# Attention probabilities of 43 steps transposed by DMA transposition on SyncE's queue, in place of TensorE transpositions and PSUM moves

## The chip, the cores and the metric

The kernel runs on the 8 cores of one Trainium2 chip, one sequence of the batch on each core, with no exchange between them. The time of a run is the device time of the slowest core in microseconds. Each core has TensorE (matmuls and transpositions), VectorE, ScalarE, GpSimd, and SyncE, which only issues DMA transfers here. GpSimd issues transfers too, mainly the weight loads, which round float32 to bfloat16 on the way.

## The reference

Two layers on x of shape (8, 2048, 1024). The change touches the attention of the first layer alone: three head groups with dilations 1, 4 and 16, four heads of 128 each.

```python
sc = jnp.einsum("brnqhe,brnkhe->brnhqk", qb, kk) * (e ** -0.5)   # (B, dil, nb, H, Q, 2Q)
...
sc = jnp.where(mask[None, None, :, None], sc, NEG_INF)
m = jnp.max(sc, axis=-1, keepdims=True)
ex = jnp.exp(sc - m)
den = jnp.sum(ex, axis=-1)                                           # (B, dil, nb, H, Q)
o = jnp.einsum("brnhqk,brnkhe->brnqhe", ex, vv) / jnp.moveaxis(den, -1, -2)[..., None]
```

Each query block of 128 positions looks at its own block of keys and the one before it. Beside the attention the layer has a gated causal convolution over 31 taps, and both feed one output projection. Then come a layer norm, a SwiGLU, an embedding, and a second layer with a short convolution.

## The kernel before

The attention is worked off in six units of two heads and one head group, and each unit in eight steps of two query blocks: 48 steps, a = 0 to 47. A step is scores(a) on TensorE into the PSUM pair PD[2], the mask and row minimum on VectorE (L1215 and L1221, in masked), four exponentials on ScalarE into Pb (L937), the transposition of P on TensorE into PSUM bank PTB[0] (transpose_p, L618), a move of it into PTt on ScalarE (steps in P_ON_ACT, L947) or VectorE (the other 16, L1233), outputs(a) on TensorE (L636), which multiplies with V, and u_move on ScalarE (L968), after which SyncE stores the block to scr (store_u, L1811). A step with two blocks of 256 keys has 8 tiles of 128x128 to transpose; a step of the group with dilation 16, or of first blocks, has 4; steps 0 and 40 have 6.

Around the steps, TensorE projects the queries, keys and values of the next unit (project, L559 and L586), whose rotary embedding is done by VectorE (L1196 to L1200) and GpSimd (L1625). In unit 0 the input of the convolution takes that place (gated, L663); later its transpositions (phases_to_rows L672, conv_back L697) and the convolution (L688). While units 3 to 5 run, the results of three groups are loaded back (load_rows, L1838 to L1845), weighted and added (merge_first L987 on ScalarE, merge L1273 and L1280 on VectorE), and transposed on TensorE (merged_back L648). The statistics go through HBM: ScalarE stores them (scs), SyncE loads them (STL, L1819), and VectorE's weights wait for that.

The order of all this is one list, EVEN, made by even_order: pairs such as ("e", a) for the exponentials, ("t", a) for the transposition, ("o", a) for outputs. Every engine walks through the same list and issues its own part in that order, so a wait holds up all that stands behind it on its engine. In units 1 to 4 the place of step a is: exponentials of a - 1, first half of a projection with outputs of a - 2 in it, second half, transposition of a - 1, scores of a. PTB[0] has one reader at a time: BANK0 lists its users, and each waits (read0) until the one before has been moved out. Pb and PTt have two buffers each.

Weight loads on GpSimd stand in its own program: load_unit for the next unit's projection (L1597), and the output projection's WmixE (L1679), each behind a rotary addition.

Of the kernel before, what the change touches and what calls it, by code (L numbers as in the profile page):

```python
# [19 lines left out]
K = 1024  # L20
# [20 lines left out]
P_ON_ACT = [*range(8, 16), *range(24, 48)]  # L41
# [144 lines left out]
def build():  # L186
# [110 lines left out]
    Pb = sb2("Pb", [128, 4, 256], BF16, off_dg0, 2 * K)  # L297
# [27 lines left out]
    def half(i):  # L325
# [16 lines left out]
    pe_s, dve_ms, dve_mn, act_exp, pe_t, dve_pt, act_pt = (sem(n) for n in (  # L342
        "pe_s", "dve_ms", "dve_mn", "act_exp", "pe_t", "dve_pt", "act_pt"))
# [142 lines left out]
    BANK0 = [u for u in EVEN if u[0] in ("t", "z", "cb", "mb")]  # L486
# [43 lines left out]
    def tensor_program(pe):  # L530
# [77 lines left out]
        def transpose_p(a):  # L608
            if a == 0:
                pe.wait_ge(dve_const, 1)  # L610
            pe.wait_ge(act_exp, 4 * a + 4)
            if a >= 1:
                pe.wait_ge(*read0(("t", a)))
            n = 0
            for bi, blk in enumerate(step_blocks(a)):
                for h in range(2):
                    for c in range(2 if qblock(UNITS[a // 8][1], blk)[0] else 1):
                        mm = pe.transpose(out=PTB[0][:, n * 128:(n + 1) * 128],  # L618
                                          in_=Pb[a % 2][:, 2 * bi + h, c * 128:(c + 1) * 128], identity=ident[:])
                        n += 1  # L620
            mm.then_inc(pe_t, 1)
# [45 lines left out]
        def phases_to_rows(c):  # L667
            if c == 0:
                pe.wait_ge(dve_glu, 16)
            pe.wait_ge(*read0(("z", c)))  # L670
# [55 lines left out]
        def even_mixer():  # L726
            for kind, v in EVEN:
# [8 lines left out]
                elif kind == "t":  # L736
# [168 lines left out]
    def scalar_program(act):  # L905
# [1131 lines left out]
```

## Time and profile before

| what | value |
|---|---|
| median of 3 runs | 1874.15 us (1873.45 to 1919.63) |
| profiled execution | 1876.64 us |
| its span, slowest core (core 2) | 1875.0 us |
| spans of the eight cores | 1864.8 to 1875.0 us |
| TensorE busy | 1768.8 us, 94% of the span |
| VectorE busy | 1076.7 us, 57% |
| ScalarE busy | 541.6 us, 29% |
| GpSimd busy | 292.7 us, 16% |
| transpositions of P on TensorE (L618) | 300, from 93.1 to 499.7 us |
| moves of P: ScalarE L947, VectorE L1233 | 32 and 16 |

The profiled execution has its own time, 1.6 us above its span and 2.5 above the median. The shares are means over the whole program; the change lies between 80 and 460 us of it, so the rows are read there, in windows. In the chain of waits each step is followed back to what released it. The queue q0 (software) carries what GpSimd issues, q1 (hardware) what SyncE issues, q10 what ScalarE issues.

### The profile page before, as it was taken

Reading aid. Unit: us, or ns where it says so; the run is one execution under the profiler, and the core shown is the slowest. Engines: PE = TensorE matmul, PEld = TensorE weight load, DVE = VectorE, ACT = ScalarE, POOL = GpSimd, SP = SyncE. Lnnn points to the kernel's source line nnn. Section 1 sums busy time; section 2 is a strip of 40 time slices with the busy share of each in tenths; the row PEclk is TensorE's granted clock in tenths of the full one; section 3 lists DMA queues with packets and bytes.
Section 4 is the critical chain, followed back from the end, with each engine's and each line's share of the span. In section 5 each row is a group of like instructions: output and inputs, shape, how many; then the busy total and the mean of one; then the engine's idle time right before and its main releaser. Section 6 shows DMA issues by size and latency. Waiting matters only on the chain.

```text
span 1875.0 us, 27051 instructions; the slowest of 8 cores (1864.8 to 1875.0 us)
## 1 busy us (share of the span) xinstructions
PE 1768.8 (94%) x9307; PEld 890.3 (47%) x9488; DVE 1076.7 (57%) x1466; ACT 541.6 (29%) x1059; POOL 292.7 (16%) x304
## 2 busy tenths in 40 slices
PE   6998989988679999999999999999899999999998
PEld 2566656555334444444444444444344444444443
DVE  3455678677695424243486675667824334156668
ACT  2341246567575010101023331113510110101223
POOL 2315443322142000000011100002300000001011
PEclk7999999999799999999999999999999999999999
DMA  9633321735342622132112426113554312330224
GB/s 284 154 66 56 63 59 45 155 105 141 135 115 59 103 40 46 34 65 48 34 23 51 74 49 120 34 34 63 69 88 85 57 23 45 57 57 12 51 74 146
DMA packets 114452, 141.63 MB, mean 76 GB/s; under 512 B 77712, under 2 KB 89104, under 8 KB 111760
## 3 DMA queue, kind: packets, MB, share of 16 engines
q0 software_dynamic: 15120, 63.84, 20.0%
q1 hardware_dynamic: 97568, 74.88, 14.9%
q10 hardware_dynamic: 1632, 1.18, 0.3%
q8 instruction: 80, 1.31, 0.3%
q14 instruction: 52, 0.43, 0.1%
HBM read 168.97 MB, written 19.01 MB: 100 GB/s over the span
## 4 chain that ended last, share of the span: by engine, by line
PE 76%; DVE 9%; issue 5%; DMA 4%; ACT 3%; POOL 1%; SPq 0%; DVEq 0%; ACTq 0%; POOLq 0%
PE pd L812 32%; PE pd L838 16%; PE pd L765 9%; PE pd L856 6%; PE pd L559 4%; PE pd L663 3%; PE pd L586 2%; DVE x_tok L1468 2%; ACT Pb L937 1%; DVE x_tok L1409 1%; DMA xf<-xT 1%; DMA Wt<-conf_conv_we 1%; PE pd L868 1%; DMA xT<-castt 1%; PE pd L602 1%
## 5 line engine op out<-in xcount | busy, mean ns | idle before, releaser
L812 PE MATMUL pd<-xT,ring 128*128 128x512 bf16 x2507 | 553.3, 379 | 10.7 <-DVE hTf L1442 3.2
L812 PEld LDWEIGHTS pd<-xT,ring 128*128 128x128 bf16 x2560 | 249.7, 98 | 310.9 <-issue 11.9
L1071 ACT ACTIVATE sgt<-pd 128x512 f32<-128x512 f32 x176 | 104.9, 597 | 690.4 <-PE pd L812 690.2
L1442 DVE TENSOR_TENSOR hTf<-pd,sgt 128x512 bf16<-128x512 f32 x128 | 88.5, 692 | 345.8 <-ACT sgt L1071 345.8
L838 PE MATMUL pd<-Wfo,hTf 128*128 128x512 bf16 x1003 | 221.1, 379 | 1.1
L1457 DVE TENSOR_TENSOR x_tok<-x_tok,pd 128x1024 f32<-128x1024 f32 x128 | 156.4, 1222 | 57.2 <-PE pd L838 56.7
L559 PE MATMUL pd<-xT,ring 128*128 128x512 bf16 x543 | 175.0, 396 | 11.2 <-DVE xT L1330 5.1
L838 PEld LDWEIGHTS pd<-Wfo,hTf 128*128 128x128 bf16 x1024 | 100.2, 98 | 120.8
L765 PE MATMUL pd<-xT,ring 128*128 128x512 bf16 x502 | 114.8, 383 | 3.7 <-DVE yT L1505 2.6
L856 PE MATMUL pd<-Wpg,x2T 128*128 128x512 bf16 x502 | 115.2, 379 | 0.7 <-DVE sigt L1483 0.2
L1588 POOL DMA_DIRECT2D ring<-ffn_w_in x40 | 21.4, 536 | 603.4 <-PE pd L812 523.7
L1196 DVE TENSOR_TENSOR rt<-pd,rope 128x512 f32<-128x512 f32 x96 | 66.1, 689 | 78.7 <-PE pd L559 32.2
L937 ACT ACTIVATE Pb<-sS,ST 128x256 bf16<-128x256 f32 (+1 forms) x192 | 86.1, 452 | 63.5 <-DVE ST L1221 63.5
L586 PE MATMUL pd<-ring,xT 128*128 128x256 bf16 x384 | 89.0, 277 | 5.3 <-DVE ring L1337 3.4
L559 PEld LDWEIGHTS pd<-xT,ring 128*128 128x128 bf16 x576 | 55.6, 101 | 76.8 <-issue 31.4
L586 PE MATMUL pd<-wx,xT 128*128 128x256 bf16 x384 | 89.1, 273 | 0.9 <-issue 0.2
L1442 DVE TENSOR_TENSOR hTq<-pd,sgt 128x512 bf16<-128x512 f32 x48 | 33.2, 691 | 92.2 <-ACT sgt L1071 92.1
L1625 POOL TENSOR_TENSOR qb<-rt,rt 128x1024 bf16<-128x1024 f32 x24 | 56.6, 2358 | 176.7 <-DVE rt L1200 170.3
L838 PE MATMUL pd<-Wfo,hTq 128*128 128x512 bf16 x376 | 83.8, 379 | 0.4
L765 PEld LDWEIGHTS pd<-xT,ring 128*128 128x128 bf16 x512 | 50.3, 99 | 64.9 <-issue 5.7
L856 PEld LDWEIGHTS pd<-Wpg,x2T 128*128 128x128 bf16 x512 | 49.9, 98 | 61.3 <-issue 2.0
L1625 POOL TENSOR_TENSOR kb<-rt,rt 128x1024 bf16<-128x1024 f32 x24 | 56.6, 2357 | 124.4 <-DVE rt L1200 124.4
(160 smaller groups left out, 2253.7 us busy)
## 6 DMA issues: line engine op xcount, KB each, us to landing
ring<-ffn_w_in POOLq DMA_DIRECT2D x40, 512.0 KB, 5.2
scr<-Ust SPq DMA_DIRECT2D x80, 128.0 KB, 2.0
Wfo<-ffn_w_out POOLq DMA_DIRECT2D x10, 1024.0 KB, 10.4
x_tok<-x SPq DMA_DIRECT2D x16, 512.0 KB, 5.4
out<-x_tok SPq DMA_DIRECT2D x15, 512.0 KB, 2.9
xf<-xT SPq DMA_DIRECT2D x3, 2048.0 KB, 21.9
ring<-even_w_in POOLq DMA_DIRECT2D x9, 512.0 KB, 8.6
La<-scr SPq DMA_DIRECT2D x11, 384.0 KB, 3.4
```

Source lines behind the costliest of these rows:

```text
L559: qk = pe.matmul(half(h % 3), lhsT=wqk[:, d, part * 128:(part + 1) * 128], rhs=xT[:, d, tc * 512:(tc + 1) * 512], start=(d == 0), stop=(d ...
L586: return pe.matmul(half(3)[:, j * 256:(j + 1) * 256], lhsT=xT[:, d, st0:st0 + 127 * dil + 1:dil], rhs=wqkv[3 * (n % 2) + 2][:, d, :], star ...
L765: mm = pe.matmul(bank, lhsT=src[:, d, j2 * 128:(j2 + 1) * 128], rhs=xT[:, d, tc * 512:(tc + 1) * 512], start=(d == 0), stop=(d == 7))
L812: mm = pe.matmul(bank[:, w * 512:(w + 1) * 512], lhsT=w_in[:, d, w * 128:(w + 1) * 128], rhs=xT[:, d, tc * 512:(tc + 1) * 512], start=(d = ...
L838: mm = pe.matmul(bank[:, hf * 512:(hf + 1) * 512], lhsT=ht, rhs=wo[:, hf * 512:(hf + 1) * 512], start=(ff == 0), stop=(ff == nf - 1))
L856: mm = pe.matmul(bank[:, hf * 512:(hf + 1) * 512], lhsT=x2T[t % 2][:, c, :], rhs=Wpg[:, c, hf * 512:(hf + 1) * 512], start=(c == 0), stop= ...
L937: act.activation(out=Pb[a % 2][:, i, 0:nk], in_=sS[a % 2][:, 2 * h + bi, 0:nk], func=AF.Exp, scale=-1.0, bias=ST[:, a // 8, sblk, 2 + h:3 ...
L1071: act.activation(out=sgt[n % 2][:], in_=PD[PAIR[l]["in", f, tc]][:, 0:512], func=AF.Silu).then_inc(act_silu, 1)
L1196: dve.tensor_tensor(out=rt1[:, part, :], in0=bank, in1=rcs[:, 0, cs], op=ALU.mult)
L1442: dve.tensor_tensor(out=ht, in0=PD[PAIR[l]["in", f, tc]][:, 512:1024], in1=sgt[n % 2][:], op=ALU.mult).then_inc(dve_h, 1)
L1457: dve.tensor_tensor(out=xt, in0=xt, in1=bank[:], op=ALU.add).then_inc(dve_acc, 1)
L1625: pool.tensor_tensor(out=(qb, kb)[i % 2][n % 2][:, :, tc * 512:(tc + 1) * 512], in0=rt1[:], in1=rt2[:], op=ALU.add).then_inc(pool_rope, 1)
```

## The change

For steps 0 to 42 the tiles of P are transposed by one DMA transposition per step, from Pb to PTt, issued by SyncE (p_back). TensorE's transpositions and the moves from PSUM are gone for these steps; steps 43 to 47 stay as they were, all moved by ScalarE. P lies packed in Pb, since one DMA takes it whole. outputs(a) now waits for d_pt, the landing of the DMA, and exponentials(a) waits for the landing of step a - 2 before it overwrites Pb. The remaining users of PTB[0] wait for one another only. In SyncE's order p_back(a) stands at the exponentials of its step for a below 33, and behind store_u(a - 2) from 33 on; 260 of the 300 tiles are in these 43 steps.

```diff
-P_ON_ACT = [*range(8, 16), *range(24, 48)]
+P_ON_PE = 43
...
-    Pb = sb2("Pb", [128, 4, 256], BF16, off_dg0, 2 * K)
+    Pb = sb2("Pb", [128, 1024], BF16, off_dg0, 2 * K)
...
-    pe_s, dve_ms, dve_mn, act_exp, pe_t, dve_pt, act_pt = (sem(n) for n in (
-        "pe_s", "dve_ms", "dve_mn", "act_exp", "pe_t", "dve_pt", "act_pt"))
+    pe_s, dve_ms, dve_mn, act_exp, pe_t, act_pt = (sem(n) for n in ("pe_s", "dve_ms", "dve_mn", "act_exp", "pe_t", "act_pt"))
+    d_pt = [sem("d_pt%d" % i) for i in range(2)]
...
-    BANK0 = [u for u in EVEN if u[0] in ("t", "z", "cb", "mb")]
+    BANK0 = [u for u in EVEN if u[0] in ("z", "cb", "mb") or u[0] == "t" and u[1] >= P_ON_PE]
...
     def moved(a):
 
-        return (act_pt, sum(b in P_ON_ACT for b in range(a + 1))) if a in P_ON_ACT else (
-            dve_pt, sum(b not in P_ON_ACT for b in range(a + 1)))
+        return (act_pt, a - P_ON_PE + 1) if a >= P_ON_PE else (d_pt[a % 2], 16 * (a // 2 + 1))
+
+    def columns(a):
+
+        return 128 * sum(4 if qblock(UNITS[a // 8][1], b)[0] else 2 for b in step_blocks(a))
...
         def transpose_p(a):
-            if a == 0:
-                pe.wait_ge(dve_const, 1)
             pe.wait_ge(act_exp, 4 * a + 4)
-            if a >= 1:
-                pe.wait_ge(*read0(("t", a)))
...
+            pe.wait_ge(*read0(("t", a)))
+            transpose_tile(Pb[a % 2], 0, columns(a) // 128).then_inc(pe_t, 1)
...
-                elif kind == "t":
+                elif kind == "t" and v >= P_ON_PE:
                     transpose_p(v)
...
         def exponentials(a):
             act.wait_ge(dve_mn, a + 1)
             if a >= 2:
-                act.wait_ge(pe_t, a - 1)
+                act.wait_ge(*((pe_t, a - 1 - P_ON_PE) if a - 2 >= P_ON_PE else moved(a - 2)))
+            n = 0
...
-                act.activation(out=Pb[a % 2][:, i, 0:nk], in_=sS[a % 2][:, 2 * h + bi, 0:nk], func=AF.Exp, scale=-1.0,
+                act.activation(out=Pb[a % 2][:, n:n + nk], in_=sS[a % 2][:, 2 * h + bi, 0:nk], func=AF.Exp, scale=-1.0,
...
-        def p_move(a):
-            if a in P_ON_ACT:
-                return
-            n = 128 * sum(4 if qblock(UNITS[a // 8][1], b)[0] else 2 for b in step_blocks(a))
-            dve.wait_ge(pe_t, a + 1)
-            if a >= 2:
-                dve.wait_ge(pe_u, a - 1)
-            dve.tensor_copy(out=PTt[a % 2][:, 0:n], in_=PTB[0][:, 0:n]).then_inc(dve_pt, 1)
...
+        def p_back(a):
+
+            sp.wait_ge(act_exp, 4 * a + 4)
+            if a >= 2:
+                sp.wait_ge(pe_u, a - 1)
+                sp.wait_ge(d_pt[a % 2], 16 * (a // 2))
+            n = columns(a)
+            sp.dma_start(out=PTt[a % 2][:, 0:n].rearrange("p (c n) -> p c n", n=128), in_=Pb[a % 2][:, 0:n],
+                         transpose=True).then_inc(d_pt[a % 2], 16)
...
         for kind, v in EVEN:
-            if kind == "o":
+            if kind == "e" and v < 33:
+                p_back(v)
+            elif kind == "o":
                 store_u(v)
+                if 33 <= v + 2 < P_ON_PE:
+                    p_back(v + 2)
```

On TensorE, where the projection of unit 3 ends (L559, L586) and that of unit 4 begins: the transpositions of step 22 (L618, reading Pb), the scores of step 23 (L602), then the transpositions of conv_back (L697, reading Zn). Before:

```order
L586 MATMUL pd<-wx_109,xT 128x256 x5
L618 MATMUL ptb<-ident,Pb_126 128x128 x8
L602 MATMUL pd<-kb_46,qb_44 128x256 x8
L697 MATMUL ptb<-ident,Zn 128x128 x8
L559 MATMUL pd<-xT,ring_104 128x512 x5
L586 MATMUL pd<-ring_106,xT 128x256
```

and in the changed kernel, where the lines are others (project L563 and L590, scores L606, conv_back L693):

```order
L590 MATMUL pd<-wx_109,xT 128x256 x5
L606 MATMUL pd<-kb_46,qb_44 128x256 x8
L693 MATMUL ptb<-ident,Zn 128x128 x8
L563 MATMUL pd<-xT,ring_104 128x512 x5
L590 MATMUL pd<-ring_106,xT 128x256
```

The eight transpositions between the projection and the scores are gone, and conv_back's follow the scores as before.

On SyncE, from the store of step 21 to the loads for the first merges: the stores of Ust (L1811), the statistics (STL), the rows La. Before:

```order
L1811 DMA scr<-Ust_141 128x256 x2
L1819 DMA STL<-scs 128x16x4 x2
L1811 DMA scr<-Ust_142 128x256 x2
L1811 DMA scr<-Ust_143 128x256 x2
L1811 DMA scr<-Ust_141 128x256 x2
L1845 DMA La_67<-scr 128x768
L1845 DMA La_68<-scr 128x768
L1842 DMA La_69<-scr 128x512
```

and in the changed kernel (stores L1796, statistics L1814, rows L1840 to L1838, transpositions L1806):

```order
L1806 DMA_TRANSPOSE PTt_136<-Pb_126 128x8x128
L1796 DMA scr<-Ust_141 128x256 x2
L1806 DMA_TRANSPOSE PTt_137<-Pb_127 128x8x128
L1814 DMA STL<-scs 128x16x4 x2
L1796 DMA scr<-Ust_142 128x256 x2
L1806 DMA_TRANSPOSE PTt_136<-Pb_126 128x4x128
L1796 DMA scr<-Ust_143 128x256 x2
L1806 DMA_TRANSPOSE PTt_137<-Pb_127 128x4x128
L1796 DMA scr<-Ust_141 128x256 x2
L1840 DMA La_67<-scr 128x768
L1840 DMA La_68<-scr 128x768
L1837 DMA La_69<-scr 128x512
```

A transposition of Pb now stands ahead of each store; the one of step 23 is ahead of the statistics' loads, which wait for the stores of ScalarE, and the ones of steps 24 and 25 are behind them.

## Rows read from the trace of the kernel before

**Rows 1.** The page's head: the span of the slowest core.

```profile
span 1875.0 us, 27051 instructions; the slowest of 8 cores (1864.8 to 1875.0 us)
```

**Rows 2.** Busy us by stage: PE, PEld, DVE, ACT, POOL; granted clock, DMA share, GB/s.

```profile
78.00:142.00 64.00, 61.76 (x390) 41.85 (x396) 32.89 (x40) 26.38 (x81) 7.64 (x6) 1.00 0.49 86
208.00:257.00 49.00, 44.29 (x306) 27.71 (x310) 37.12 (x75) 17.74 (x64) 19.45 (x13) 1.00 0.25 55
257.00:352.00 95.00, 91.14 (x698) 62.21 (x712) 73.55 (x111) 56.31 (x144) 31.61 (x18) 0.98 0.34 72
390.00:480.00 90.00, 70.17 (x593) 43.13 (x604) 66.43 (x117) 64.92 (x191) 19.39 (x9) 0.96 0.45 127
```

**Rows 3.** TensorE's timeline, step 21: start us, us, engine, line, operation.

```profile
318.71 0.61 PE L618 MATMUL ptb<-ident,Pb 128*128 128x128 bf16 x8
319.25 1.09 PE L602 MATMUL pd<-kb,qb 64*128 64x256 bf16 x8
```

**Rows 4.** Waits, 257 to 352 us (total, times, longest); a wait in TensorE's timeline.

```profile
PE ptb L697 <- DVE PTt L1233: 2.1, 7, 0.6
...
256.98 0.38 PE L618 MATMUL ptb<-ident,Pb 128*128 128x128 bf16 x4 [2.29 <-ACT Pb L937]
```

**Rows 5.** Landing of 28 x2T transpositions; DMA queues from 1046 to 1050 us.

```profile
DMA to landing us min/median/max: 3.0/3.1/4.2
...
q0 software_dynamic: 174, 0.65, 101.7%
q1 hardware_dynamic: 37, 0.00, 1.0%
xT<-castd SPq DMA_TRANSPOSE x1, 9.5
```

**Rows 6.** Loads issued by GpSimd and transfers beside them (last column: us to landing).

```profile
268.94 1.72 POOL L1597 DMA_DIRECT2D ring<-even_w_in  x3
...
ring<-even_w_in POOLq DMA_DIRECT2D x3, 512.0 KB, 11.4
...
355.24 0.57 POOL L1679 DMA_DIRECT2D WmixE<-even_w_out  x1
...
WmixE<-even_w_out POOLq DMA_DIRECT2D x1, 2048.0 KB, 17.7
scr<-Ust SPq DMA_DIRECT2D x2, 128.0 KB, 16.0
```

**Rows 7.** Steps 15, 23, 26: last exponential L937, outputs L636; scores(26) L602.

```profile
269.93 0.39 ACT L937 ACTIVATE Pb<-sS,ST 128x128 bf16<-128x128 f32 x1
...
276.56 0.39 PE L636 MATMUL ptb<-Vb,PTt 128*128 128x128 bf16 x4
...
332.96 0.49 ACT L937 ACTIVATE Pb<-sS,ST 128x256 bf16<-128x256 f32 x1
...
338.42 0.61 PE L636 MATMUL ptb<-Vb,PTt 128*128 128x128 bf16 x8
349.06 1.15 PE L602 MATMUL pd<-kb,qb 64*128 64x128 bf16 x8
...
355.50 0.39 ACT L937 ACTIVATE Pb<-sS,ST 128x128 bf16<-128x128 f32 x1
...
359.83 0.39 PE L636 MATMUL ptb<-Vb,PTt 128*128 128x128 bf16 x4
```

**Rows 8.** The chain of waits from 330 to 365 us: start us, us, what.

```profile
333.68 9.20 DMA scs<-ST
...
353.49 0.70 DVE ST L1221
...
360.53 0.70 DVE ST L1221
```

**Rows 9.** Busy time from 250 to 270 us, columns as in rows 2.

```profile
250.00:260.00 10.00, 7.71 (x49) 4.39 (x48) 7.72 (x17) 3.09 (x11) 3.06 (x3) 0.92 0.10 35
260.00:270.00 10.00, 9.73 (x64) 6.29 (x65) 7.17 (x14) 4.46 (x18) 5.73 (x4) 0.91 0.08 28
```

More of the change, by code:

```diff
@@ L608, in transpose_p @@
         def transpose_p(a):
-            if a == 0:
-                pe.wait_ge(dve_const, 1)
             pe.wait_ge(act_exp, 4 * a + 4)
-            if a >= 1:
-                pe.wait_ge(*read0(("t", a)))
[L614 to L621, printed above, removed]
+            pe.wait_ge(*read0(("t", a)))
+            transpose_tile(Pb[a % 2], 0, columns(a) // 128).then_inc(pe_t, 1)
         def outputs(a):
@@ L668, in phases_to_rows @@
             if c == 0:
+                pe.wait_ge(dve_const, 1)
                 pe.wait_ge(dve_glu, 16)
-            pe.wait_ge(*read0(("z", c)))
+            else:
+                pe.wait_ge(*read0(("z", c)))
             for i in range(8):
@@ L896, in tensor_program @@
         for i in range(WARM):
-            pe.matmul(PD[2][:, 0:512], lhsT=Pb[1][:, 0, 0:128], rhs=Pb[1][:, 0:2, :].rearrange("p a b -> p (a b)"),
+            pe.matmul(PD[2][:, 0:512], lhsT=Pb[1][:, 0:128], rhs=Pb[1][:, 0:512],
                       start=True, stop=True)
@@ L936, in exponentials @@
                 sblk = st_block(UNITS[a // 8][1], blk)
-                act.activation(out=Pb[a % 2][:, i, 0:nk], in_=sS[a % 2][:, 2 * h + bi, 0:nk], func=AF.Exp, scale=-1.0,
+                act.activation(out=Pb[a % 2][:, n:n + nk], in_=sS[a % 2][:, 2 * h + bi, 0:nk], func=AF.Exp, scale=-1.0,
                                bias=ST[:, a // 8, sblk, 2 + h:3 + h],
                                accum_out=ST[:, a // 8, sblk, h:h + 1]).then_inc(act_exp, 1)
+                n += nk
         def p_move(a):
-            if a not in P_ON_ACT:
-                return
-            n = 128 * sum(4 if qblock(UNITS[a // 8][1], b)[0] else 2 for b in step_blocks(a))
-            act.wait_ge(pe_t, a + 1)
+            n = columns(a)
+            act.wait_ge(pe_t, a - P_ON_PE + 1)
             act.wait_ge(pe_u, a - 1)
@@ L1050, in even_mixer @@
                     exponentials(v)
-                elif kind == "t":
+                elif kind == "t" and v >= P_ON_PE:
                     p_move(v)
@@ L1224, in masked @@
             d.then_inc(dve_mn, 1)
-        def p_move(a):
-            if a in P_ON_ACT:
-                return
-            n = 128 * sum(4 if qblock(UNITS[a // 8][1], b)[0] else 2 for b in step_blocks(a))
-            dve.wait_ge(pe_t, a + 1)
-            if a >= 2:
-                dve.wait_ge(pe_u, a - 1)
-            dve.tensor_copy(out=PTt[a % 2][:, 0:n], in_=PTB[0][:, 0:n]).then_inc(dve_pt, 1)
         def merge_weights(batch):
@@ L1376, in even_mixer @@
                     masked(v)
-                elif kind == "t":
-                    p_move(v)
                 elif kind == "z":
```

1 line of the change is left out of this document (added).

## Prediction

> **What bounds the kernel now.** I first read the span [rows 1]: the profiled execution took 1876.64 us, of which 1875.0 are the span of its slowest core, and the median of the runs shown is 1874.15, so 2.5 less; I sum against 1876.64 and take 2.5 off at the end. All 43 changed steps lie between 80 and 460 us. There the sums by stage [rows 2] show four regimes. From 78 to 142 us (gate and convolution input) TensorE is busy 61.8 of 64 us and VectorE half: TensorE bounds. From 208 to 257 us VectorE works 37 of 49 us with GpSimd beside it, and TensorE stands waiting for exponentials at the end [rows 4]: the rotary chain bounds. From 257 to 352 us TensorE is busy 91.1 of 95 us: it bounds again. From 390 to 480 us TensorE, VectorE and ScalarE have 70, 66 and 65 of 90 us, and none is full: a loop of waits bounds. From 352 to 390 us it is the same kind of loop: the chain of waits goes from one row-minimum (L1221) to the next in 7.04 us by VectorE and ScalarE alone, with no transposition in it [rows 8].
>
> **What the change removes.** 260 of the 300 transpositions leave TensorE, and 43 moves from PSUM leave VectorE (16) and ScalarE (27). Eight transpositions delay the score matmuls behind them by 319.25 - 318.71 = 0.54 us [rows 3], that is 0.0675 us each. Where TensorE bounds this is all gain, where it does not it is nothing:
> - Steps 0 to 5, 46 transpositions before 142 us: 3.1 us.
> - Steps 6 and 7, 16 of them, ahead of the first convolution matmuls: 1.1 us.
> - Steps 8 to 13, 24 of them, under the rotary chain: 0.
> - Steps 14 to 22, 56 of them, TensorE bound: 3.8 us.
> - The conv_back transpositions in that stage waited for the bank that VectorE's move of P still read: 2.1 us over 7 times [rows 4]; the bank is now free: 2.1 us.
> - Step 13's transposition held TensorE 2.29 us for the exponentials [rows 4]. TensorE can now go on with the scores; it bounds from here, so 2.3 us.
> - Steps 23 to 30, 36 of them, under the loop: 0.
> - Steps 31 to 42, 82 of them, and with them the ScalarE moves: between 0 and 5.5 us. The loop runs by VectorE and ScalarE; I take 1.0, near the lower end, since [rows 8] is the nearest row for such a loop and it holds no move.
>
> The sum of the gains is 3.1 + 1.1 + 3.8 + 2.1 + 2.3 + 1.0 = 13.4 us. The removed moves on VectorE and ScalarE are otherwise idle-covered.
>
> **What it adds.** 43 DMA transpositions, on SyncE's queue, each issued when the last exponential of its step is done; outputs(a) on TensorE waits for the landing, and behind that wait stand on TensorE the rest of the projection and the scores two steps on; behind outputs stand u_move on ScalarE, then merge_first, then VectorE's merge and its next mask: everything. exponentials(a) waits for the landing of step a - 2, which is an old one by then. In quiet, such a transposition of 128x1024 lands in 3.0 to 4.2 us, median 3.1 [rows 5]. What is there to cover it is the time from the last exponential to outputs: 276.56 - 270.32 = 6.2 us for step 15, 338.42 - 333.45 = 5.0 for step 23, 359.83 - 355.89 = 3.9 for step 26 [rows 7], less the 0.3 to 0.8 us by which TensorE now comes earlier. So in quiet the landing is hidden, by 0.0 to 2.5 us. In steps 0 to 7 two whole steps of gated blocks lie between, which is more cover than in any later one.
>
> It is not always quiet. While a weight load issued by GpSimd runs, the hardware queues hardly move: in the 4 us from 1046 to 1050 the software queue took 101.7% of the 16 engines with 174 packets, the hardware queue 1.0% with 37, and the transposition then under way landed after 9.5 us [rows 5]. Beside the WmixE load two stores of 128 KB each needed 16.0 us [rows 6]. So I take it that a transposition issued just before or in such a load lands at the load's end. Three steps are hit in the TensorE-bound or loop-bound part:
> - Step 15: last exponential 270.32 [rows 7], loads issued from 268.94 on, the last at about 270.1, landing 11.4 us later at 281.5 [rows 6], and the transposition 1.5 us behind it at 283.0. TensorE would be at outputs(15) at 276.56 less 0.27 for four transpositions and 0.3 for the bank, 276.0: it stalls 7.0 us.
> - Step 23: the scs store issued at 333.68, right behind its exponentials, took 9.20 us beside the next loads, to 342.88 [rows 8]; the transposition then lands at about 343.2. TensorE is at outputs(23) at 338.42 - 0.54 = 337.9: 5.3 us.
> - Step 26: WmixE is issued at 355.24, 0.65 us ahead of the last exponential, and lands after 17.7 us [rows 6], at 372.9. outputs(26) was at 359.83: 13.2 us late.
>
> After a stall the clock is lower: around the 2.29 us wait that ended at 256.98 the mean granted clock was 0.92 from 250 to 260 and 0.91 from 260 to 270 [rows 9], which is (0.08 + 0.09) x 10 = 1.7 us of work lost in a stretch at 1.2 instead of 2.4 GHz. I add 1.7 per stall. Step 15 lies where TensorE bounds: 7.0 + 1.7 = 8.7 us. For step 23, scores(26) moves from 349.06 [rows 7] to 349.06 + 343.2 - 338.42 + 1.7 - 0.5 = 355.0, and ends at 356.2; its mask started 0.7 us before the minimum at 353.49, so 352.8 [rows 8]; the slack was 2.6 us, and the loop slips 3.4. For step 26: 13.2 + 1.7 - 0.3 (its neighbour's transpositions) - 2.6 (the same slack) = 12.0 us. Together 24.1 us. The bounds of this sum are 0 (all three hidden) and, if each lands 3 us later still, 33.
>
> Ahead of step 24's transposition stands, on SyncE, the wait for the scs store and the STL loads; it lands at about 350, when TensorE, late by step 23, has just come to outputs(24). I count nothing for it, but without step 23's stall it would cost what that one does.
>
> **The forecast.** 24.1 - 13.4 = 10.7 us slower: 1887.3 for an execution like the profiled one, 1885 at the median. That is 0.6%, where 2% is about what a measurement of this kernel tells from no change.
>
> **Rivals.**
> First, the load at 269 us misses step 15. Its data starts some 2 us after its issue, and the transposition follows it by only 1.4 us; with four transpositions gone ahead of it, it is 0.3 us earlier still. Against it: the load would have to leave it 3.1 us. Then the sum is 24.1 - 8.7 - 13.4 = +2.0, at the median 1876. Chance 0.18.
>
> Second, the queues share. A transposition of 3.1 us beside a load then takes twice that, 6.2: step 15 lands at 276.5 (0.5 late), step 23 at 339.7 and step 26 at 362.1, late by 1.8 and 2.3, within the slack of 2.6. With one lowered clock the losses are about 2.2 us, the sum is -11.2, and the median comes to 1863. For it: the hardware queue did move some packets beside the load. Against it: 37 packets against 174 [rows 5], and the 16.0 us of the stores [rows 6]. Chance 0.2. The Trainium skill, page "DMA: Bandwidth & Descriptors", section "Issuing engines are not separate DMA queues", says that DMAs from all issuing engines interleave on the same 16 engines, which is this rival; by it the median would be 1863, and [rows 5] and [rows 6] speak against it.
>
> Third, slower by over 2%. From step 8 to step 30 the cover is 3.9 to 6.2 us [rows 7], about 4.5 after TensorE comes earlier. If the ordinary landing, behind the stores of Ust and the loads of La on the same queue, is not 3.1 but 7 us, each of 20 steps stalls 2.5 us: 50 us more, on top of the forecast 1935. It decides from a landing of about 4.5 us on. Against it: all 28 transpositions of x2T landed in 4.2 us or less [rows 5]. Chance 0.06.
>
> That the transpositions stay on TensorE is ruled out by the order of the changed program.
>
> **How the numbers follow.** Forecast (all three stalls) 0.48; first rival 0.18; second 0.2; third 0.06; other mixtures (one stall alone, or two) 0.08, between 1866 and 1882. The range goes from below the second rival, 1861, to the forecast with each landing 3 us later less half the doubt of the gains, 1896; it leaves out the third rival and half of the second's better end. Faster by over 2% would be 1837, which no case reaches: 0.01. Slower by over 2%: 0.06. Within: 0.93.
>
> **What would show it.** Transpositions of P land in 3 to 4 us except those of about steps 8, 15, 23 and 26, which land after 9 to 17 us; TensorE waits for PTt before outputs(15), (23) and (26), the last one some 13 us long, each followed by a stretch at half the granted clock; a step with its two gated blocks, from 78 to 142 us, takes 0.54 us less; conv_back follows the scores with no gap; from 352 us on everything is later than before by about 11 us. The forecast is wrong if no wait for PTt is over 3 us (then the second rival), or if most steps from 8 on wait (the third).

## The result, and the profile after

The changed kernel took 1893.86 us in the median of five runs (1889.92 to 2069.55), the kernel before 1874.15. Runs in which the cores of a die went at a visibly lower clock, like the one of 2069.55 us, are left out of the ratios here and of the medians given below. The ratio is 1.0096, with a 95% interval of 1.0082 to 1.011: about 18 us slower, and within 2%. The profiled execution took 1891.94 us, 15.3 more than the one before; its slowest core is again core 2.

The head of the changed kernel's page, and from the list of its DMA issues the row of the 43 new ones (number, median us to landing):

```profile
span 1889.8 us, 26667 instructions; the slowest of 8 cores (1876.0 to 1889.8 us)
...
PTt<-Pb SPq DMA_TRANSPOSE x43, 3.1
```

The median landing is that of the other transpositions, 3.1 us [rows 5]. So the median says nothing is wrong, and the spread has to be looked at. All instructions on the tile PTt: what TensorE waited for before its outputs (us in all, times), who waited for it, and the spread of the landings:

```profile
  DMA PTt<-Pb: 40.9, 9
...
  PE ptb L630: 42.4, 10
  ACT Ust L964: 27.5, 4
...
DMA to landing us min/median/max: 2.4/3.1/16.0
```

At nine of the 43 steps TensorE waited, 40.9 us together. TensorE's timeline says which (start, us, what; in brackets the idle time ahead and what ended it; L630 is outputs). They are steps 2, 12, 15, 23, 26, 35, 37 and 39; a ninth, of 0.6 us, is left out:

```profile
117.23 1.01 PE L630 MATMUL ptb<-Vb,PTt 128*128 128x128 bf16 x8 [3.76 <-DMA PTt<-Pb]
...
249.51 0.38 PE L630 MATMUL ptb<-Vb,PTt 128*128 128x128 bf16 x4 [2.26 <-DMA PTt<-Pb]
...
281.03 0.59 PE L630 MATMUL ptb<-Vb,PTt 128*128 128x128 bf16 x4 [9.91 <-DMA PTt<-Pb]
...
345.19 1.01 PE L630 MATMUL ptb<-Vb,PTt 128*128 128x128 bf16 x8 [6.04 <-DMA PTt<-Pb]
...
378.22 0.58 PE L630 MATMUL ptb<-Vb,PTt 128*128 128x128 bf16 x4 [10.78 <-DMA PTt<-Pb]
...
440.82 0.61 PE L630 MATMUL ptb<-Vb,PTt 128*128 128x128 bf16 x8 [2.08 <-DMA PTt<-Pb]
...
453.12 0.61 PE L630 MATMUL ptb<-Vb,PTt 128*128 128x128 bf16 x8 [2.33 <-DMA PTt<-Pb]
...
464.24 0.61 PE L630 MATMUL ptb<-Vb,PTt 128*128 128x128 bf16 x8 [3.11 <-DMA PTt<-Pb]
```

Four of them stand in the chain of waits with the whole flight of their DMA (start us, us, what), and each was issued beside weight loads of GpSimd; for step 15 GpSimd's row is the first here:

```profile
266.23 1.72 POOL L1582 DMA_DIRECT2D ring<-even_w_in  x3
```

```profile
100.84 16.04 DMA PTt<-Pb
...
267.15 13.54 DMA PTt<-Pb
...
334.75 10.10 DMA PTt<-Pb
...
363.06 14.81 DMA PTt<-Pb
```

Busy time by stage, to be read against [rows 2] (columns as there):

```profile
78.00:142.00 64.00, 60.24 (x339) 38.14 (x339) 27.68 (x33) 25.05 (x76) 7.64 (x6) 0.97 0.65 107
208.00:257.00 49.00, 45.35 (x283) 25.89 (x282) 37.24 (x78) 16.15 (x60) 17.90 (x10) 0.97 0.33 72
257.00:352.00 95.00, 79.05 (x567) 51.77 (x566) 61.43 (x83) 50.56 (x126) 29.41 (x18) 0.91 0.46 91
390.00:480.00 90.00, 75.07 (x534) 42.43 (x532) 68.59 (x124) 52.08 (x177) 21.21 (x9) 0.94 0.58 127
```

The third line shows it best: TensorE's 91.1 busy us of 95 are now 79.1, and its granted clock 0.91 in place of 0.98. A part of the fall is the transpositions that are gone, the rest comes from the waits of 9.9 and 6.0 us. VectorE, which had nothing taken away in the last stage, is nearly the same there (68.6 and 66.4 us), though the later windows no longer hold quite the same steps.

One core is not enough for sizes of 2 or 3 us. So I took, on each of the eight cores, the start of TensorE's scores of steps 0, 8, 14, 24, 32, 41 and 46 and of the first convolution matmul, and the median of the eight for each stretch between two of them. Names e1 to e12 are the experiments below.

| us, median of 8 cores | steps 0-7 | convolution | 8-13 | 14-23 | 24-31 | 32-40 | 41-45 |
|---|---|---|---|---|---|---|---|
| before | 73.0 | 57.6 | 45.8 | 77.8 | 56.0 | 48.8 | 37.6 |
| after | 70.2 | 56.4 | 45.5 | 80.6 | 73.2 | 48.8 | 36.6 |
| e1 eight steps back | 70.5 | 56.8 | 42.8 | 74.9 | 58.1 | 49.7 | 35.9 |
| e2 four alone | 73.0 | 55.7 | 45.8 | 84.9 | 72.9 | 48.9 | 36.9 |
| e3 paced loads | 69.6 | 56.3 | 42.8 | 73.2 | 59.4 | 50.7 | 35.8 |
| e4 none late | 70.5 | 55.9 | 42.8 | 74.9 | 57.5 | 48.9 | 37.8 |
| e5 0-22, paced | 69.6 | 56.2 | 42.8 | 73.5 | 55.5 | 48.8 | 37.3 |
| e6 0-22, 39-42, paced | 69.6 | 56.2 | 42.8 | 73.5 | 55.9 | 48.6 | 36.2 |
| e7 load shifted | 70.3 | 55.8 | 42.8 | 80.2 | 71.5 | 49.6 | 36.5 |
| e8 four plain copies | 72.9 | 55.9 | 45.8 | 81.9 | 71.7 | 48.9 | 37.5 |
| e9 before, paced | 73.0 | 56.5 | 45.8 | 77.8 | 55.0 | 48.8 | 37.6 |
| e10 unpaced, 23 steps | 70.5 | 57.0 | 42.8 | 74.9 | 56.2 | 48.7 | 36.2 |
| e11 load in 1 KB | 70.4 | 55.7 | 42.8 | 81.5 | 68.9 | 50.5 | 36.2 |
| e12 load in 512 B | 70.8 | 55.6 | 43.8 | 81.9 | 67.2 | 48.8 | 36.7 |

The wait of a step comes two steps later than its scores, so that of step 23 falls in the stretch 24-31. The convolution waits for its own weights too and differs by 1.2 to 6.0 us from core to core within a kernel; nothing is read from it. Without any DMA in its steps, the stretch 24-31 has medians of 55.0 to 56.2 us in five kernels (before, e5, e6, e9, e10), so differences under about 1 us say nothing there. What follows scores(46) differs by 3 to 10 us from core to core within a kernel, so the time of a whole run, which is that of its last core, says less about the change than the stretches do. Differences in the text are taken before rounding and can be 0.1 us off those of the table. The stretches 14-23 and 24-31 hold the loss: +2.9 and +17.1 us.

### The profile page after: what moved, and what is told of

Same layout as the page of the kernel before. It is cut to its first block, busy times and chain, and to the rows that moved or that the text cites. A ratio compares the mean times of both kernels' runs of the same rounds, so it can differ in the third digit from the quotient of the medians.

```text
span 1889.8 us, 26667 instructions; the slowest of 8 cores (1876.0 to 1889.8 us)
## 1 busy us (share of the span) xinstructions
PE 1772.5 (94%) x9228; PEld 875.5 (46%) x9228; DVE 1067.2 (56%) x1450; ACT 526.3 (28%) x1032; POOL 293.1 (16%) x304
## 4 chain that ended last, share of the span: by engine, by line
PE 74%; DVE 9%; DMA 7%; issue 4%; ACT 3%; POOL 2%; SPq 0%; DVEq 0%; ACTq 0%; POOLq 0%
PE pd L808 31%; PE pd L834 16%; PE pd L761 9%; PE pd L852 5%; PE pd L563 4%; DMA PTt<-Pb 4%; PE pd L657 2%; PE pd L590 2%; DVE x_tok L1453 2%; DVE x_tok L1394 1%; DMA xf<-xT 1%; PE pd L864 1%; ACT Pb L934 1%; DMA Wt<-conf_conv_we 1%; DMA xT<-castt 1%
## 5 line engine op out<-in xcount | busy, mean ns | idle before, releaser
L808 PE MATMUL pd<-xT,ring 128*128 128x512 bf16 x2560 | 556.3, 379 | 8.9 <-DVE hTf L1427 3.2
L563 PE MATMUL pd<-xT,ring 128*128 128x512 bf16 x576 | 186.1, 399 | 9.5 <-ACT xT L921 6.0
L1442 DVE TENSOR_TENSOR x_tok<-x_tok,pd 128x1024 f32<-128x1024 f32 x128 | 156.4, 1222 | 57.0 <-PE pd L834 56.8
L761 PE MATMUL pd<-xT,ring 128*128 128x512 bf16 x512 | 113.8, 379 | 3.2 <-DVE yT L1490 2.6
L934 ACT ACTIVATE Pb<-sS,ST 128x256 bf16<-128x256 f32 (+1 forms) x192 | 86.2, 452 | 71.7 <-DVE ST L1217 66.6
L590 PE MATMUL pd<-ring,xT 128*128 128x256 bf16 x384 | 90.8, 282 | 5.6 <-DVE ring L1324 3.9
L563 PEld LDWEIGHTS pd<-xT,ring 128*128 128x128 bf16 x576 | 56.2, 101 | 76.5 <-issue 31.9
L590 PE MATMUL pd<-wx,xT 128*128 128x256 bf16 x384 | 91.2, 278 | 0.0
```

Of the source, the lines that this page charges most:

```text
L563: qk = pe.matmul(half(h % 3), lhsT=wqk[:, d, part * 128:(part + 1) * 128], rhs=xT[:, d, tc * 512:(tc + 1) * 512], start=(d == 0), stop=(d ...
L590: return pe.matmul(half(3)[:, j * 256:(j + 1) * 256], lhsT=xT[:, d, st0:st0 + 127 * dil + 1:dil], rhs=wqkv[3 * (n % 2) + 2][:, d, :], star ...
L761: mm = pe.matmul(bank, lhsT=src[:, d, j2 * 128:(j2 + 1) * 128], rhs=xT[:, d, tc * 512:(tc + 1) * 512], start=(d == 0), stop=(d == 7))
L808: mm = pe.matmul(bank[:, w * 512:(w + 1) * 512], lhsT=w_in[:, d, w * 128:(w + 1) * 128], rhs=xT[:, d, tc * 512:(tc + 1) * 512], start=(d = ...
L934: act.activation(out=Pb[a % 2][:, n:n + nk], in_=sS[a % 2][:, 2 * h + bi, 0:nk], func=AF.Exp, scale=-1.0, bias=ST[:, a // 8, sblk, 2 + h:3 ...
L1442: dve.tensor_tensor(out=xt, in0=xt, in1=bank[:], op=ALU.add).then_inc(dve_acc, 1)
```

## The experiments

Theory A is that of the prediction: a transposition issued beside a weight load of GpSimd lands when the load does, little else costs, and the gains on TensorE are real. The rival B is that the new DMAs cost by themselves, wherever they stand. Unless said otherwise the kernel before took 1873.2 to 1874.0 us beside these runs.

**e1, eight steps back.** The steps beside loads go back to TensorE and a move from PSUM; the semaphore counts and the users of PTB[0] follow the list.

```diff
-P_ON_PE = 43
+BY_DMA = [0, 1, 4, 5, 6, 7, 8, 9, 10, 11, 12, 13, 14, 17, 18, 19, 20, 21, 22, 25, 28, 29, 30, 31, 32, 33, 34, 35, 36, 37, 38, 39, 40, 41, 42]
...
-                elif kind == "t" and v >= P_ON_PE:
+                elif kind == "t" and v not in BY_DMA:
                     transpose_p(v)
```

> The changed kernel with eight of its 43 steps given back to TensorE and the PSUM move: 2, 3, 15, 16, 23, 24, 26 and 27, those whose transposition was issued beside a weight load of GpSimd. 35 stay with the DMA. Theory A (a transposition beside a load lands at the load's end, and nothing else costs): the 40.9 us of waits for PTt shrink to the three short ones of steps 35, 37 and 39 (7.5 us) and those at 240 and 250 us, and what is left are the gains: steps 0, 1, 4, 5 2.0 us, 6 and 7 1.1, 14 and 17 to 22 about 3.2, the bank of conv_back 1.5, step 13 2.3, together 10: about 1864 us against 1874. Theory B (any transposition by this queue costs about what the changed kernel lost, by the order of SyncE's instructions or by stores on the same queue): the waits move to neighbouring steps and the time stays at 1880 us or above.

Measured: 1864.21 and 1867.17 us, two runs and so without an interval, 8 us below the kernel before. The tile PTt, waits of TensorE and landings:

```profile
  DMA PTt<-Pb: 13.6, 9
...
DMA to landing us min/median/max: 2.4/3.1/10.7
```

35 DMAs are left, and of 40.9 us of waits 13.6, none over 2.7 us. The stretch 24-31 falls from 73.2 to 58.1, and 14-23 from 80.6 to 74.9. B would have kept the loss. But 58.1 is still 2 us above before. A part of it is a step beside a load that the list of eight missed. In this kernel WmixE was on its way from 344.6 to 362.7 us, and the transposition of step 28 was issued at 360.1, as its row in the chain of waits says:

```profile
360.09 6.20 DMA PTt<-Pb
```

TensorE waited 2.69 us for it, and in the median of the eight cores 2.9 us. The other wait in the stretch is that of step 25, 1.7 us (median 1.4), with no load beside it. The transposition of step 0 was also issued beside a load, an earlier one, and landed after 10.7 us; its cover hid it.

**e2, four alone.** The reverse: `BY_DMA = [2, 15, 23, 26]`, everything else as before.

> The kernel before with only steps 2, 15, 23 and 26 transposed by DMA; the other 44 stay with TensorE and the move (the five steps of this group that VectorE moved before still by VectorE). Theory A: these four carry the whole loss. The changed kernel ended 18 us later with gains of about 11, so its losses are about 29; less 1.9 for the 28 transpositions gone: 1874 + 27 = about 1901 us, with waits for PTt of about 10, 6 and 11 us before outputs(15), (23) and (26) and about 4 before outputs(2). Theory B (the loss is spread over the 43 steps): 1880 us or below.

Measured: 1898.15 us, ratio 1.013 (1.0113 to 1.0148). Four DMAs cost 24.5 us, more than the 43 together. TensorE's timeline, the waits of steps 15, 23 and 26:

```profile
280.51 0.58 PE L642 MATMUL ptb<-Vb,PTt 128*128 128x128 bf16 x4 [8.68 <-DMA PTt<-Pb]
...
349.73 1.01 PE L642 MATMUL ptb<-Vb,PTt 128*128 128x128 bf16 x8 [5.87 <-DMA PTt<-Pb]
...
381.76 0.58 PE L642 MATMUL ptb<-Vb,PTt 128*128 128x128 bf16 x4 [9.96 <-DMA PTt<-Pb]
```

The 4 us expected before outputs(2) didn't come on this core; three others waited 1.2 to 2.9 us, and in the median steps 0-7 take 73.0 as before. Step 2 hurts only where its cover happens to end first: in the changed kernel steps 0-7 take 75.1 us on core 2 and 69.6 to 71.2 on the other seven.

**e3, paced loads.** All 43 by DMA; the load is cut, and each piece waits for a landing.

```diff
+                if 2 <= n < 5 and i < 3:
...
+                    pool.wait_ge(*moved(8 * n - 8 + i))
+                    load_part(n + 1, i)
...
-                if n == 4 and i == 2:
+                if n == 4 and 3 <= i < 7:
                     pool.wait_ge(pe_bt, 8)
-                    pool.dma_start(out=WmixE[:], in_=ewout_d).then_inc(d_wmix, 16)
+                    pool.wait_ge(*moved(24 + i))
+                    pool.dma_start(out=WmixE[:, 2 * i - 6:2 * i - 4], in_=ewout_d[:, 2 * i - 6:2 * i - 4]).then_inc(d_wmix, 16)
```

> The changed kernel, all 43 steps by DMA, with GpSimd's weight loads cut in pieces of 512 KB and each piece issued only when the transposition of a step has landed: q, k and v of units 3, 4 and 5 after the transpositions of steps 8, 9, 10, then 16, 17, 18, then 24, 25, 26; WmixE in four pieces after those of steps 27 to 30; in unit 0 one piece after each of steps 2 to 6. Theory A: a piece alone needs about 4 us and ends before the next transposition, or delays it by 2 us at most, which the cover of 4 to 6 us takes: no wait for PTt over 3 us from step 2 to step 30, and about 1862 us. Theory B: the waits stay, 1885 us or above. A third outcome, the pieces collide with each following transposition: several waits of 2 to 4 us each, 1875 to 1890.

Measured: 1871.6 us, ratio 0.999 (0.9978 to 1.0001): between the first and the third outcome. Steps 0 to 23 come out as A says, the best of all kernels (69.6, 42.8, 73.2). The loss is in the loop, 59.4 us against 56.0, where small waits follow one another. Here a piece of a load is under way beside nearly every step, and the transpositions of steps 25 to 30 landed after 4.4 to 5.2 us on this core, not after 2.4 as beside no load. Two of the waits from TensorE's timeline:

```profile
349.25 0.38 PE L630 MATMUL ptb<-Vb,PTt 128*128 128x128 bf16 x4 [2.44 <-DMA PTt<-Pb]
...
364.35 0.38 PE L630 MATMUL ptb<-Vb,PTt 128*128 128x128 bf16 x4 [1.33 <-DMA PTt<-Pb]
```

**e4, none late.** As e1, with steps 33 to 42 on TensorE too: `BY_DMA` ends at 32.

> The first of these kernels with steps 33 to 42 given back to TensorE and ScalarE's move as well: 25 steps are left to the DMA. The prediction gave steps 31 to 42 a gain of 1.0 us (0 to 5.5). If that is right, this kernel is about 1 us slower than the first one, 1865. If the short waits of steps 35, 37 and 39 (2.1 to 3.1 us) cost more than the removed moves gain, it is 2 to 7 us faster, 1857 to 1862.

Measured: 1868.1 us, ratio 0.9973 (0.9962 to 0.9984). The times of e1 and e4 don't settle it (two runs of e1). The stretches do better: 32-40 takes 48.9 us against 49.7, 41-45 37.8 against 35.9. What the DMA gains at the end of the attention it partly loses ahead of it.

**e5, steps 0 to 22, loads of units 1 to 4 paced.** The load of unit 5 and WmixE go back to their places, steps 23 to 47 to TensorE.

> Steps 0 to 22 by DMA, steps 23 to 47 by TensorE and ScalarE's move; the loads of units 1 to 4 cut in three pieces, each issued after the landing of a step's transposition, as in the paced kernel; the load of unit 5 and WmixE whole and where they were. By the stage medians over eight cores, theory A (the gain lies where TensorE bounds and in the waits of step 13, and the small landing waits of steps 25 to 31 cost 1.4 to 3.4 us in the loop) gives 73.0 - 69.6 = 3.4 us for steps 0 to 7, 3.0 for steps 8 to 14, 4.5 for 15 to 22, and nothing lost after: 1873.7 - 10.9 = about 1863 us. Theory B (what the paced kernel lost from step 24 on came from later starts elsewhere, not from the DMA of those steps) keeps 1868 to 1871.

Measured: 1866.3 us, ratio 0.9966 (0.9952 to 0.9981), 3 us above A's number in the time. The stretches agree with A: 3.5, 3.0 and 4.3 us gained, and 24-31 back at 55.5. So the DMAs of steps 23 to 31 do cost 1.4 to 3.4 us in the loop (e4, e1, e3). That they cost it with no load beside them is not shown: in e1 and e4 the largest wait is that of step 28, beside the end of WmixE (median 2.9 and 2.8 us), and in e3 the pieces stand beside them. What is left for a step with no load near is the wait of step 25, 1.4 and 1.1 us in the median of e1 and e4. The eight spans of the profiled execution, one of the quicker ones with 1862.4 us, were 1850.8 to 1860.8 us, against 1864.8 to 1875.0 before; the last one counts.

**e6, steps 39 to 42 as well.**

> As the kernel with steps 0 to 22 by DMA and paced loads, and steps 39 to 42 by DMA as well, each issued behind the store two steps before. In all kernels with those steps by DMA the stretch from scores(41) to scores(46) took 35.8 to 36.6 us in the median of the cores, in the two kernels without 37.6 and 37.8. If this is theirs, it comes again here: about 1.5 us less than with steps 0 to 22 alone, 1861 to 1862. If it came from earlier steps or from chance, no difference.

Measured: 1864.8 us, ratio 0.9955 (0.9937 to 0.9972). 41-45 takes 36.2 us on all eight cores against 37.3 in the median of e5: the 1.1 us are theirs. The times of e5 and e6 alone don't tell them apart.

**e7, one load shifted.** The changed kernel with this on GpSimd:

```diff
-            if n < 5:
+            if n < 5 and n != 3:
                 load_unit(n + 1)
...
+                if n == 3 and i == 2:
+                    load_unit(4)
```

> The changed kernel with one edit on GpSimd: the load of unit 4's weights is issued after the third rotary addition of unit 3 instead of before the first, some 20 us later. Theory A (a transposition beside a load lands at the load's end): the wait of 9.9 us before outputs(15) is gone, and one of 4 to 9 us stands before outputs(18) or (19) instead; the time is that of the changed kernel within 5 us, 1887 to 1896. Theory B (step 15 is slow for a reason of its own, such as the stores before it): the wait stays at step 15.

Measured: 1890.3 us, ratio 1.0088 (1.0072 to 1.0104). The load in GpSimd's timeline:

```profile
283.34 1.72 POOL L1582 DMA_DIRECT2D ring<-even_w_in  x3
```

TensorE's timeline; the first row is step 17, the second step 18:

```profile
284.16 0.38 PE L630 MATMUL ptb<-Vb,PTt 128*128 128x128 bf16 x4 [0.39 <-DMA PTt<-Pb]
297.32 1.01 PE L630 MATMUL ptb<-Vb,PTt 128*128 128x128 bf16 x8 [6.00 <-DMA PTt<-Pb]
```

Step 15 waits no longer, step 18 waits 6.0 us. It is so on all eight cores: no wait for PTt before outputs(15), and 5.0 to 8.3 us before outputs(18). The stall follows the load. This is the sharpest evidence for A: nothing at step 15 was changed.

**e8, four plain copies.** As e2, without `transpose=True`: P of these four steps reaches PTt untransposed.

> The kernel with only steps 2, 15, 23 and 26 by DMA, and in these the DMA is a plain copy from Pb to PTt of the same bytes, not a transposition, so that the output of these steps is not the reference's. If it is the hardware queue that stands still beside a GpSimd load (theory A), the copies land as late as the transpositions did (10 to 14 us), and the time is 1896 to 1900. If it is the transposition, with its many small packets (theory B), the copies land within 5 us and the time is 1873 to 1877.

Measured: 1896.6 us, ratio 1.0123 (1.0106 to 1.0139). The tile PTt (TensorE's waits, then the landings):

```profile
  DMA PTt<-Pb: 19.3, 3
...
DMA to landing us min/median/max: 8.7/9.6/13.9
```

A plain copy of 128 or 256 KB needs 8.7 to 13.9 us there too. No run has such a copy away from a load; the nearest are two plain stores of 128 KB on the same queue from 298.5 to 302 us of the changed kernel, which landed after 2.0 us. The transposition adds to it: at step 15 TensorE waited 8.68 us for it and 4.74 for the copy, which is the row below (in the median of the cores 7.1 and 4.2), and 14-23 takes 84.9 and 81.9. In the traces the transposition of step 15 is 512 packets of 256 bytes, the copy 128 packets of 1 KB. So it is the queue beside the load that is slow, whatever it carries, and by a lesser part the transposition's many packets.

```profile
276.85 0.58 PE L642 MATMUL ptb<-Vb,PTt 128*128 128x128 bf16 x4 [4.74 <-DMA PTt<-Pb]
```

**e9, the kernel before with paced loads.** A control for e5 and e6.

> The kernel before, with all transpositions on TensorE, and only the loads of units 1 to 4 cut and paced as in the kernel with steps 0 to 22 by DMA (each piece issued when the P of a step has been moved). It tells what of that kernel's gain is the pacing's. Theory A: nothing, 1873 to 1875 us, and steps 0 to 7 take 73.0, 8 to 14 45.75 and 15 to 22 77.8 us as before. Theory B: the pacing itself lets the stage run quicker: 1866 or below.

Measured: 1873.8 us, ratio 1.0004 (0.9993 to 1.0015). The pacing alone gives nothing.

**e10, unpaced.** `BY_DMA = [0, 1, 4, ..., 14, 17, ..., 22, 39, 40, 41, 42]`, the loads untouched.

> Loads whole and where they were, and the DMA only for steps 0, 1, 4 to 14, 17 to 22 and 39 to 42, 23 in all: no step beside a load. Beside the kernel with steps 0 to 22 and 39 to 42 by DMA and paced loads it gives up steps 2, 3, 15 and 16, which the stage medians put at 0.9 us (70.46 against 69.56) and 1.4 us (74.88 against 73.46). Theory A: 1873.5 - 7.7 = about 1866 to 1867 us. If it is as fast as the paced one (1864.8) or faster, the pacing isn't worth its code.

Measured: 1864.8 us, ratio 0.9955 (0.9941 to 0.9969), the same as e6. It gives up 0.9 and 1.4 us in two stretches, and the times don't show them. Of the versions that beat both kernels this one is the simplest: 23 steps by DMA, none beside the loads that stalled TensorE (step 0's landed after 9.0 us beside an earlier one, hidden), and of the loop of VectorE and ScalarE only steps 39 to 42.

**e11 and e12, smaller pieces.** The DMA queues of the changed kernel, while WmixE was loaded beside step 26: packets, MB, time of the packets as a share of 16 engines, first from 370 to 372, then from 372 to 374 us:

```profile
q0 software_dynamic: 26, 0.43, 99.9%
q1 hardware_dynamic: 26, 0.01, 2.5%
...
q0 software_dynamic: 28, 0.46, 107.3%
q1 hardware_dynamic: 29, 0.01, 2.8%
```

In these stretches the hardware queue did not stand still. It sent as many packets as the software queue, but those are 0.46 MB / 28 = 16 KB long, and its own a few hundred bytes. Beside the load of unit 5, in pieces of 4 KB, three queues kept equal step; from 341 to 343 us:

```profile
q0 software_dynamic: 94, 0.38, 94.1%
q1 hardware_dynamic: 95, 0.02, 9.2%
q10 hardware_dynamic: 93, 0.01, 3.2%
```

This gives a third theory: the queues alternate packet by packet, and a queue of small packets is slowed by the size of the other's. Both kernels are the changed one, with the load of WmixE cut by columns, in two or four:

```diff
-                    pool.dma_start(out=WmixE[:], in_=ewout_d).then_inc(d_wmix, 16)
+                    for c in range(2):
+                        pool.dma_start(out=WmixE[:, :, c * 512:(c + 1) * 512], in_=ewout_d[:, :, c * 512:(c + 1) * 512]).then_inc(d_wmix, 16)
```

> The changed kernel, all 43 steps by DMA, with one edit: WmixE is loaded by two transfers of half the columns each, back to back, so that its pieces are 1 KB long and no longer 16 KB. In the trace of the changed kernel q0 and q1 sent packets in equal number while both had work (28 and 29 from 372 to 374 us, 26 and 26, 21 and 20), but those of q0 are 16 KB each. Theory A (the queues alternate packet by packet, so the transposition is slowed by the size of the load's packets): the transposition of step 26 lands some 6 to 8 us after its issue in place of 14.8, the wait of 10.8 us before outputs(26) falls to 0 to 4 us, those of steps 15 and 23 stay, and the time is 1880 to 1886 us. Theory B (the hardware queue stands still until the load is done, however it is cut): the wait stays at 10 to 13 us and the time at 1889 to 1894.

> As the one with pieces of 1 KB, with WmixE in four transfers of a quarter of the columns, in pieces of 512 bytes. Theory A: 4096 packets; the transposition of step 26 lands in 4 to 7 us, the wait before outputs(26) is 0 to 2 us, 1879 to 1884 us, unless the longer writing of descriptors by GpSimd holds its rotary additions. Theory B: as before, 10 us or more.

Measured: 1888.0 us with 1 KB (ratio 1.0088, 1.005 to 1.0125) and 1887.3 with 512 bytes (1.0076, 1.0046 to 1.0106). Step 26 in TensorE's timeline with 1 KB, and with 512 bytes:

```profile
371.87 0.58 PE L630 MATMUL ptb<-Vb,PTt 128*128 128x128 bf16 x4 [8.12 <-DMA PTt<-Pb]
```

```profile
372.21 0.59 PE L630 MATMUL ptb<-Vb,PTt 128*128 128x128 bf16 x4 [4.90 <-DMA PTt<-Pb]
```

The queues with 1 KB, in a stretch of 2 us in the load, 368 to 370 us:

```profile
q0 software_dynamic: 292, 0.29, 87.0%
q1 hardware_dynamic: 297, 0.10, 37.9%
```

The wait goes 10.8, 8.1, 4.9 us with the size of the load's pieces (in the median of the eight cores 10.5, 6.2, 4.5), and the stretch 24-31 73.2, 68.9, 67.2, while nothing is taken from the load. Nor does the transposition land with the load any more: in e11 it landed at 371.4 us and the load's second half at 380.5. Theory B, that the queue stands still until the load is done, is out. The Trainium skill, page "DMA: Bandwidth & Descriptors", section "Queues, rings and completion order", says that each DMA engine goes round the queues that have work and takes a whole packet from each. The equal counts agree. The sizes fall short of what I expected, 0 to 4 us with 1 KB and 0 to 2 with 512 bytes, and so do the times: they lie 4 to 5 us below the changed kernel's, but the intervals of the three ratios overlap, so it is the stretch and the waits that show the effect and not the time. The theory is right in direction and was too hopeful in size. Cutting also slows the load itself, whose last piece landed 22 us after the first issue in both and not after 15.2, so what the transposition gains by smaller packets and what it gains by a slower load is not separated.

The theory also leaves out a first part. In the changed kernel, from 366 to 368 us, the queues show one row, though the transposition had been issued at 363.06:

```profile
q0 software_dynamic: 16, 0.26, 93.8%
```

The hardware queue sent nothing. From the issue of the transposition of step 26 to its first packet of 256 bytes it took 4.8 us in the median of the cores, 4.1 and 4.2 in e11 and e12, and 1.15 us at step 18, beside no load. For step 23 it was 4.0 us, and for the plain copy in its place (e8) 3.9. So about 3 us of each of these landings come before any packet, whatever the load is cut into and whatever the queue carries. The alternation doesn't explain them. At step 26 what stands ahead on the same queue, the stores of Ust and a load of La of 384 KB, may be a part of it. The cause of this first part stays open.

## Why the prediction was right, and where not

1885 us was forecast, 1893.86 came, within the range of 1861 to 1896 and on the forecast's side: three stalls beside loads, and a gain that they outweigh. The sum was +10.7 us; the seven stretches of the table give +14.6, with -1.3 of the convolution among them, which I read nothing into. The gains were sized about right: undisturbed they are 3.5 + 3.0 + 4.3 + 1.4 = 12.2 us (e6 against before) for 13.4. The losses came out larger, about 28 us for 24.1 (the changed kernel against e6): 17.2 in the stretch 24-31, 7.2 in 14-23, 2.7 in 8-13 by a late landing at step 12 that was not in the sum, and 0.6 in the first. So the time landed near the upper end of the range. Term by term:

- **Steps 0 to 7**, forecast -4.2 (3.1 and 1.1). With no load in their way -3.5 (e3, e5, e6), so the price of 0.0675 us for a transposition held to within a fifth. In the changed kernel -2.9, and +2.1 on the core that ended last. The step that failed is "which is more cover than in any later one", from which I concluded that no load matters there. The cover was 12.6 us, the most indeed, and the landing 16.0: I compared the cover with the covers of other steps and not with the length of the load.
- **Steps 8 to 13**, forecast -2.3 for the wait of step 13. Undisturbed it is -3.0. In the changed kernel two of the eight cores have it whole and one 1.9 us of it, and the median is -0.3. On core 2 the 2.26 us before outputs(12) took it, by a landing of 4.1 us in place of 2.4 (below); the six cores that lack it or a part of it are the six with such a landing. Step 8, which the signs named as one of the late ones, landed after 4.2 us on core 2 and cost nothing.
- **Steps 14 to 23**, forecast +8.7 - 3.8 - 2.1 = +2.8, measured +2.9. The gain was 4.3 and not 5.9 (e5 against before), and the stall cost 7.2 and not 8.7. The wait itself was 9.9 us on core 2 (8.3 in the median), not 7.0. My landing was right: 14.1 us from the load's issue to the end of the wait forecast, 281.03 - 266.23 = 14.8 measured. TensorE was earlier: 4.9 us behind the load's issue (281.03 - 9.91 - 266.23), where I had 276.0 - 268.94 = 7.1. The load hangs on VectorE's rotary chain, and TensorE had gained on that chain. What an engine gains just ahead of a stall, the stall takes back. That the sum came out at +2.9 is luck: two errors cancelled.
- **Steps 24 to 31**, forecast 3.4 + 12.0 = +15.4, measured +17.1. The waits were 6.0 and 10.8 us for 5.3 and 13.2, since WmixE landed after 15.2 us and not 17.7. The clock cost more than the 1.7 us that I took for each: see the rows below. The slack of 2.6 us was taken off for step 23 and again for step 26; without the second the sum would be 18.0, and no run shows whether it was there twice. And "hidden by 0.0 to 2.5 us" was too kind for the loop: with the large loads cut in pieces beside them the landings cost 3.4 us there (e3), which steps on TensorE give back (e5). In the changed kernel that part is covered by the stalls: with four DMAs alone the stretch takes 72.9 us (e2).
- **Steps 31 to 42**, forecast -1.0, measured 0.0 and -1.0. The waits of 2.1 to 3.1 us before outputs(35), (37) and (39) were not foreseen, but before the change TensorE's place was taken by ScalarE's move: e4, with that move, waits 1.1 to 1.9 us at the same places. The term was sized right for the wrong steps: it comes from 39 to 42 (e6).

Granted clock (the number ahead of the last two) of TensorE in the 5 us behind the waits of steps 15, 23 and 26, and in an undisturbed stretch:

```profile
281.00:286.00 5.00, 4.97 (x24) 0.65 0.19 61
...
291.00:300.00 9.00, 9.00 (x68) 1.00 0.17 45
...
345.00:350.00 5.00, 4.80 (x23) 0.56 0.60 66
...
378.00:383.00 5.00, 4.78 (x18) 0.50 0.50 152
```

That is 5 us at 0.65, 0.56 and 0.50, so 1.8, 2.2 and 2.5 us of work lost at or near the lower level of 1.2 GHz. In the 5 us after these the granted clock is 1.00, 1.00 and 0.95.

Of the rivals, the first (the load misses step 15) and the third (an ordinary landing of 7 us) did not happen; the ordinary one stayed at 3.1. The second, that the queues share, was dismissed with "the hardware queues hardly move". As to time that was right, since bytes hardly moved; as to the reason it was half right. Once a transposition's packets run they alternate evenly with the load's, and then the sizes decide, which my rival had left out. But the 37 packets against 174 are not from such a stretch. The last transposition of xT was issued at 1045.2 us, and of the 37 packets only 5, all after 1049, are of 256 bytes; the other 32 carry 4 bytes each. Those 4 us lie in the first part, before a transposition's packets begin, and there the queue did hardly move.

## What to carry to other kernels

A transfer that replaces work on an engine needs cover against the slowest moment of its queues, not against its median landing: here the landings of four steps beside weight loads cost 24.5 us alone, more than all the others gave back. List the large loads with their times first, leave the steps beside them on the engine, and change only the steps in stages that this engine bounds; 23 of the 43 steps gave 0.9955 where all gave 1.0096. And place a stall relative to what triggers the load, not to the old time of the waiting engine.

## What the runs showed of the hardware

The DMA queues of GpSimd and SyncE send packets in equal number once both have packets under way: 26 to 26 and 28 to 29 with 16 KB on GpSimd's side, 94 to 95 with 4 KB, 292 to 297 with 1 KB, and 256 bytes to some KB on SyncE's. Before that comes a gap: the first packet of a transposition or copy issued beside a load came 3.9 to 5.4 us after its issue (steps 15, 23 and 26, medians of the cores), against 1.15 us beside none. A plain copy of 128 KB landed after 9.6 us beside a load of three times 512 KB. Cutting a load of 2 MB into pieces of 1 KB or 512 bytes let the transposition beside it through 2.7 or 5.9 us sooner on the slowest cores (medians of the eight: 14.6, 10.2 and 8.6 us to landing).

A landing can also be late with no load of the kernel in sight. On core 2, from 241 to 250 us, the DMA queues and the issues (last column: us to landing) show step 12's transposition and one packet of an instruction queue:

```profile
q8 instruction: 1, 0.02, 0.9%
...
PTt<-Pb SPq DMA_TRANSPOSE x1, 4.1
```

On core 2 the transposition from 236 to 241 us, with no such packet beside it, took 2.4. Ten kernels have step 12 by DMA (the changed one, e1, e3 to e7 and e10 to e12), so there are 80 traces of cores. In 18 of them, six in the changed kernel, one such packet of 16 KB started 1.7 to 2.4 us after the issue, and the landing took 4.0 to 4.4 us; in the other 62 there was none before the landing, and it took 2.4 or 2.5 us. At step 10 of the changed kernel such a packet started 0.3 to 0.6 us after the issue, ahead of the transposition's own packets, and the landing took 2.4 to 2.6 us on all eight cores. So a single packet of that queue among a transposition's own goes, at step 12, with 1.5 us or more of delay without exception; that it is the cause is the likely reading, and no experiment moved it.
